# Two weight tiles at a time for the second feed-forward layer of token block A

## The reference

```python
x = x + jnp.einsum('bte,ed->btd', mix, p['w_out'])
h2 = rmsnorm(x, p['norm_ffn_g'])
u = jnp.square(jax.nn.relu(jnp.einsum('btd,df->btf', h2, p['w_up'])))   # first layer, 1024 -> 4096
x = x + jnp.einsum('btf,fd->btd', u, p['w_down'])                       # second layer, 4096 -> 1024
```

## Time and profile before

| | us |
|---|---|
| median of three runs | 1408.15 (1405.77 to 1410.62) |
| the profiled execution | 1409.37 |
| its span, first to last instruction | 1407.6 |
| PE busy | 1357.2, 96% of the span |
| PE idle ahead of its products for `dl` (line 2111) | 6.7, in 4 places |
| feed-forward of block A (eight groups) | about 488 to 990 of the span |

### The profile page before, as it was taken

The page is one execution under the profiler, slowest core; times in us unless marked ns, Lnnn a source line. Parts: engine busy times, 40 slices in busy tenths (PEclk is TensorE's granted clock), DMA queues, the critical chain, the costliest instruction groups (busy, mean ns, idle before and its releaser), DMA issues.

```text
span 1407.6 us, 23885 instructions
## 1 busy us (share of the span) xinstructions
PE 1357.2 (96%) x8589; PEld 1123.8 (80%) x8589; DVE 912.2 (65%) x1624; ACT 576.2 (41%) x1069; POOL 399.9 (28%) x395
## 2 busy tenths in 40 slices
PE   8899999999999999999999999999999999999998
PEld 6767777786777777777767767667999999999998
DVE  5459667755657787648667564535376665877875
ACT  6445333314545654523234232323444454334533
POOL 2546615335533545243000000000242212220220
PEclk9999999999999999999999999999999999999999
DMA  8547745344345564577386675874455563223021
GB/s 273 152 119 224 232 130 174 117 149 137 100 140 163 196 223 148 162 251 250 122 271 221 193 255 171 286 237 143 165 191 181 176 224 106 105 106 119 32 91 61
DMA packets 125543, 239.29 MB, mean 170 GB/s; under 512 B 13601, under 2 KB 46658, under 8 KB 125426
## 3 DMA queue, kind: packets, MB, share of 16 engines
q1 hardware_dynamic: 116226, 213.64, 46.0%
q10 hardware_dynamic: 9200, 24.13, 5.0%
HBM read 197.64 MB, written 40.09 MB: 169 GB/s over the span
## 4 chain that ended last, share of the span: by engine, by line
PE 53%; DVE 10%; ACT 4%; issue 3%; DMA 3%; SPq 1%; POOL 0%; ACTq 0%; DVEq 0%; POOLq 0%
PE ps L85 15%; PE ps L87 14%; PE ps L86 14%; PE ps L3298 2%; PE ps L1495 2%; PE ps L1532 2%; DVE fl L2788 2%; DMA raw_dn<-in_w_down 1%; PE ps L1314 1%; DVE uw_l L2018 1%; DMA vr<-in_cache_v 1%; DVE uw_l L2627 1%; DVE part_l L2826 1%; ACT uw_h L2012 1%; DVE xt L2835 1%
## 5 line engine op out<-in xcount | busy, mean ns | idle before, releaser
L3063 POOL TENSOR_TENSOR kr<-kr,qb 128x512 f32<-128x512 f32 x128 | 171.5, 1353 | 171.1 <-DMA kr<-in_cache_k 171.1
L85 PE MATMUL ps<-x2hB,uw_h 128*128 128x264 f32 (+1 forms) x512 | 145.7, 284 | 1.6 <-DVE x2lB L2850 0.7
L86 PE MATMUL ps<-x2lB,uw_h 128*128 128x264 f32 (+1 forms) x512 | 144.6, 282 | 0.0
L87 PE MATMUL ps<-x2hB,uw_l 128*128 128x264 f32 (+1 forms) x512 | 144.4, 282 | 0.0
L85 PE MATMUL ps<-part_h,fh 128*128 128x264 f32 (+1 forms) x448 | 128.7, 287 | 4.0 <-DVE xt L2835 3.7
L87 PE MATMUL ps<-part_h,fl 128*128 128x264 f32 (+1 forms) x448 | 126.9, 283 | 0.0
L86 PE MATMUL ps<-part_l,fh 128*128 128x264 f32 (+1 forms) x448 | 126.8, 283 | 0.0
L85 PE MATMUL ps<-uh,dh 128*128 128x512 f32 x256 | 105.1, 411 | 8.7 <-DVE dl L2111 6.7
L3052 DVE TENSOR_REDUCE sd<-kr 128x8 f32<-128x512 f32 x128 | 84.9, 675 | 36.9 <-POOL kr L3063 36.9
L2835 DVE TENSOR_TENSOR xt<-xt,ps 128x264 f32<-128x264 f32 (+1 forms) x224 | 86.2, 420 | 33.4 <-PE ps L87 33.1
L85 PE MATMUL ps<-x2hA,uw_h 128*128 128x512 f32 x256 | 105.2, 411 | 0.0
(11 more groups left out here) (383 smaller groups left out, 3442.7 us busy)
## 6 DMA issues: line engine op xcount, KB each, us to landing
kr<-in_cache_k SPq DMA_DIRECT2D x128, 256.0 KB, 3.2
raw_up<-in_w_up_units SPq DMA_DIRECT2D x64, 512.0 KB, 4.8
vr<-in_cache_v SPq DMA_DIRECT2D x128, 256.0 KB, 3.5
raw_dn<-in_w_down SPq DMA_DIRECT2D x32, 512.0 KB, 6.3
raw_dn<-in_w_down ACTq DMA_DIRECT2D x32, 512.0 KB, 4.7
raw<-in_w_in_units SPq DMA_DIRECT2D x23, 512.0 KB, 5.3
raw_up<-in_w_out_units SPq DMA_DIRECT2D x16, 512.0 KB, 4.2
kept_up_low<-uw_l SPq DMA_DIRECT2D x14, 512.0 KB, 6.6
```

The costliest lines, as they stand in the source:

```text
L85: pe.matmul(out, lh, rh, start=first and n == 0, stop=False, skip_group_check=onto)
L86: pe.matmul(out, lh, rl, start=False, stop=False, skip_group_check=onto)
L87: ins = pe.matmul(out, ll, rh, start=False, stop=last and n == len(ks) - 1, skip_group_check=onto)
L3063: pool.tensor_tensor(k[:, :], k[:, :], qb[v // PAGES][:, :], ALU.mult).then_inc(k_multiplied, 1)
```

## The change

The `w_down` tiles are taken two at a time. ACT makes the high parts of tiles x and x + 1 ahead of x = 0 and of x = 2 and none ahead of x = 1 and x = 3; DVE makes the low parts in the same way. `load_down` becomes `load_pair(n)`, which stands behind `split_high` of x = 0 and x = 2 and ahead of the square of the hidden tile: it loads tiles n and n + 1 (each waits for the low part of the tile two before it) and then stores the low parts of tiles n - 2 and n - 1, where before each store stood ahead of a load. The number of instructions of each kind is the same.

```diff
-        def load_down(n):
-
-            act.wait_ge(dn_low, n - 1)
+        def load_pair(n):
+
+            for i in (n, n + 1):
+                act.wait_ge(dn_low, i - 1)
+                f = i % (FT * FGROUPS) * P
+                act.dma_start(raw_dn[:, i % 2, :], a["w_down"][f:f + P, :]).then_inc(dn_in[i % 2], 16)
             if n == 2:
                 act.wait_ge(dn_out, STORED)
-            last = slice(0, HALF if (n - 2) % FT < 2 else D_MODEL)
-            if n - 2 < FT * KEPT_GROUPS:
-                act.dma_start(a["dn_low"][n - 2, :, last], dl[:, (n - 2) % FT, last].bitcast(FP32)).then_inc(dn_out, 16)
-            f = n % (FT * FGROUPS) * P
-            act.dma_start(raw_dn[:, n % 2, :], a["w_down"][f:f + P, :]).then_inc(dn_in[n % 2], 16)
+            for i in (n - 2, n - 1):
+                last = slice(0, HALF if i % FT < 2 else D_MODEL)
+                if i < FT * KEPT_GROUPS:
+                    act.dma_start(a["dn_low"][i, :, last], dl[:, i % FT, last].bitcast(FP32)).then_inc(dn_out, 16)
...
             for x in range(FT):
                 t = KT + FT * g + x
-                if x:
-                    load_down(FT * g + x + 1)
-                down_high(g, x)
+                if x % 2 == 0:
+                    down_high(g, x)
+                    down_high(g, x + 1)
                 beside(tick + 2 * x)
...
                 if x + 1 < FT and t > KT:
                     split_high(act, t + 2)
+                if x % 2 == 0:
+                    load_pair(FT * g + x + 2)
                 i = up_no(g, x)
...
             for o in range(KT):
-                if o == 0:
-                    load_down(FT * g + FT + 1)
                 beside(tick + 2 * FT + o)
...
                 beside(tick + 2 * x)
-                down_low(g, x)
+                if x % 2 == 0:
+                    down_low(g, x)
+                    down_low(g, x + 1)
```

## The result

| | before | after |
|---|---|---|
| median, us | 1408.15 (5 runs) | 1417.72 (1415.78 to 1420.43, 5 runs) |
| the profiled execution | 1409.37 | 1415.78 |
| its span | 1407.6 | 1414.1 |
| PE waits for `dl`, 480 to 1000 us | 6.7 in 4 places | none |

The changed kernel is slower: 1.0063 of before, interval 1.0048 to 1.0077 (the two medians of the table alone give 1.0068). The forecast was 1407.2 in a range of 1402.6 to 1411.5. The kernel lost 9.6 us between the medians and 6.4 between the two profiled executions; the profiled one of after was the fastest of its five.

What follows compares the result with a forecast made beforehand. PE, busy 96% of the span, bounds the kernel; its dl waits put 6.7 us at stake. Groups' gains and losses (-1.0, -0.85, +1.55, 0, +1.3) sum to 1.0 us faster: 1408.4 profiled, 1407.2 median, range 1402.6 to 1411.5.

Steps and rivals of the forecast that it cites:

- the ledger of groups 0 and 1: Forecast as seen by PE: group 0 loses 1.0 us (late attention copy), group 1 loses 0.85 us.
- step 2: Pair at x = 0: DVE's extra dl is covered; in group 0 the norm comes 1.1 us later, taken as 0 net.
- group 1's two delays: Group 1: 0.75 us at the score product, 0.95 at the attention product; 1.7 lost against 1.36 won.
- step 1: Head of down in groups 1, 2, 3, 5: PE's wait for the low part goes; up to 6.7 us back.
- step 3: Pair at x = 2, groups 0 to 3: DVE's relu, split_low and hidden low part come 1.14 us later.
- step 4: Four ACT issues before the square, groups 0 to 3: 0.6 to 0.75 us uncovered; at x = 2, 1.75 us later altogether.
- the estimate: Shared DVE/POOL port lock: 0.85 us more at x = 2 of groups 0, 1, 2, making the sum about 1.5 slower.
- Slower: ACT is held at x = 2: Rival, groups 0 to 3: ACT's queued work waits, 10 us lost against at most 5.6 back; 1412.6 us, chance 0.10.
- Most of it comes back: Rival: most of the 6.7 us of dl waits returns, 5.6 us in groups 1, 2, 3, 5; 1402.6 us, chance 0.18.
- the order of the transfers: Rival that only transfer order matters: early loads shorten nothing; no time of its own, lies in the forecast, no separate chance.

Runs made afterwards that it cites:

- run 6: Kernel before; only DVE's low part of tile 3 moved ahead of the side jobs of x = 3, groups 1 to 7; 1411.33 us, ratio 1.0007.
- run 8: Kernel before; tile 3's split put behind the hidden tile of x = 2 in groups 2 to 7, in group 1 DVE's low part before side jobs; 1412.63 us.
- run 1: Changed kernel with load_pair moved behind the hidden tile's copy and the side jobs, splits still in pairs; 1418.2 us, ratio 1.0051.
- run 3: Changed kernel with pairs only for tiles 0 and 1, tiles 2 and 3 as before; 1412.91 us, ratio 1.0023 to the kernel before.
- run 7: Changed kernel plus unused matmuls (14, 18, 18, 18 calls) ahead of four waiting products in groups 0 and 1; 1417.44 us, ratio 1.0063.
- run 9: Changed kernel plus unused matmuls (7, 9, 9, 9 calls) ahead of four waiting products in groups 0 and 1; 1418.31 us, ratio 1.0063.
- run 2: Changed kernel with each store again ahead of its load, at the changed place; 1416.88 us, ratio 1.0058.
- run 13: Changed kernel with group 0 as before and pairs from group 1 on; 1413.41 us, ratio 1.0023 to the kernel before.
- run 4: Changed kernel with pairs only for tiles 2 and 3, tiles 0 and 1 as before; 1413.79 us, ratio 1.0028 to the kernel before.
- run 12: Changed kernel with pairs in groups 2, 4, 5, 6, 7 only, plus seven unused matmuls in the wait at 512 us; 1409.88 us, ratio 1.0011.
- run 5: Changed kernel with groups 0 and 1 as before and pairs from group 2 on; 1409.51 us against 1409.46, ratio 1.0002.
- run 10: Changed kernel with pairs in groups 2, 4, 5, 6 and 7 only, the others as before; 1407.66 us, ratio 0.9993.

## Why the prediction was wrong, step by step

The sum forecast a gain of 1.0 us; the block lost 7.2. The step that failed is the ledger of groups 0 and 1: with step 2's "0 net" and group 1's two delays side by side it forecast -1.85, and the traces show -8.1. Beside it, group 1's 1.36 us from step 1 were counted as won and were not. By group, in the profiled executions (the measured numbers are differences between the starts of the first-layer products of one group and the next):

| group | forecast | measured | what differs |
|---|---|---|---|
| 0 | -1.0 | -2.7 | the attention copy is 3.3 later, not 1.75 |
| 1 | -0.85 | -5.5 | chain of ACT and DVE later at each turn, residual add, clock |
| 2 | +1.55 | +0.5 | 2.1 at the head, 1.6 lost in its `down` |
| 3 | 0 | -1.1 | `ul` wait of 2.29 (1.1 forecast), clock behind it |
| 5 | +1.3 | +1.1 | as said |
| 4, 6, 7 | 0 | +0.3 | |

**Step 1 was right in what it says and wrong in what it is worth.** The wait for `dl` is gone everywhere. But runs 6 and 8 take it away by other means and gain nothing, because the residual add, which hangs on POOL's products with the cached keys, is next: in run 6 the `dl` waits fall by 5.0 us and those for `xt` rise by 5.4. Group 1's 1.36 us are not worth 1.36. The prediction saw this wait and let it keep its place; it had to be moved up with PE.

**Step 2 asked the wrong engine.** The 1.1 us at the norm came (2.10 - 0.88 = 1.22), but not by DVE, where the norm "stands behind" the pair: DVE's first step of the norm began 8.4 us after the start of the first-layer products, before 8.6. It came by POOL. Timelines of DVE and POOL, before and then after:

```profile
494.98 0.27 POOL L1608 TENSOR_SCALAR stat<-stat 128x1 f32<-128x1 f32 x1
...
498.71 2.01 POOL L2104 TENSOR_TENSOR norm<-norm,half 128x4 f32<-128x4 f32 x1 [1.23 <-DVE norm L2116]
```

```profile
495.05 2.35 DVE L2113 TENSOR_TENSOR dl<-raw_dn,dh 128x1024 fp32r<-128x1024 f32 x2
495.06 2.47 POOL L1608 TENSOR_SCALAR stat<-stat 128x1 f32<-128x1 f32 x1
...
498.47 1.95 POOL L3067 TENSOR_TENSOR kr<-kr,qb 128x512 f32<-128x512 f32 x1
500.37 1.01 POOL L2106 TENSOR_TENSOR norm<-norm,half 128x4 f32<-128x4 f32 x1
```

A small POOL instruction that began with the pair ended with it, after 2.47 us instead of 0.27, and POOL's part of the norm, behind it and a key product, ended 12.1 us after the start instead of 10.9. In runs 1, 3, 7 and 9 the same instruction took 2.17 to 2.39 us; in run 2 a key product came first, and the pair took 3.18. In runs 6 and 13, with group 0 as before, it took 1.12, and the norm waited 1.41 and 1.31 us.

The prediction set these 1.1 us against the wait at 512.44, "0 net". For PE that came true: the wait at 512.44 and the slow product behind it are gone, and PE stood ready for the next attention product at 33.9 us against 34.1. But the copy that this product needs comes out of ACT and DVE, and DVE began the `dl` of x = 2 at 519.68 - 489.26 = 30.4 us instead of 519.04 - 489.85 = 29.2. Ahead of that `dl` DVE has idle time of its own (1.66 us, before 1.62), and it absorbed nothing, for the sum there waits for POOL, and POOL for a page of keys. The sums behind the norm began at 19.2 us instead of 17.4, SP's page loads wait for them, and SP issued the one for that page at 22.8 instead of 20.9. I let idle time of PE absorb a delay that ran on along DVE, SP and POOL. Run 3, which has the norm late and x = 2 as before, shows it without the second `dl`: its `dl` begins 30.3 us after the start, and the copy ends 34.4 us after it, 1.1 later than before.

```profile
520.49 1.22 DVE L2130 TENSOR_TENSOR dl<-raw_dn,dh 128x1024 fp32r<-128x1024 f32 x1
...
523.99 0.58 ACT L1567 ACTIVATE attn_t<-ps 128x512 f32<-128x512 f32 x1
```

What it costs PE beside the pair at x = 2 is less: `down` of group 0 starts 0.5 us later than before in run 3, 2.4 in run 4 and 2.7 with both.

**Steps 3 and 4 were right in mechanism.** Of the 3.3 us at group 0, 1.2 are the later start of the `dl`, 1.15 the second `dl` and 1.0 the issues (step 4 said 0.6). Run 4, with the norm as before, has the `dl` 0.7 us late and the copy 3.1, so not all of the 1.2 is the norm's; POOL's product, which waits for the page of cached keys, stands ahead of it. Step 4's figure at x = 0 is to be seen in group 1. Timeline of ACT:

```profile
577.38 0.82 ACTq L2036 DMA_DIRECT2D raw_dn<-in_w_down  x2
578.24 0.94 ACTq L2042 DMA_DIRECT2D kept_dn_low<-dl  x2
579.22 0.63 ACT L2083 ACTIVATE xr<-xr 128x512 f32<-128x512 f32 x1 [0.80 <-issue]
```

0.80 against 0.75 forecast, and the wait for `p1b` grew by 0.91 (1.75 to 2.66). By the times of run 1 the issues are not the larger part.

**The sum over group 1 failed.** The forecast put two delays beside each other and took the 1.36 off them. In the trace they follow one another on one chain, from which PE's gain at `down` takes nothing off: the attention copy of 600 comes 5.5 us later from the start than before (110.6 against 105.1): 2.7 carried from group 0, 0.9 by the issues, 0.95 by the second `dh`, and 1 us by the hidden tile's low part at 591.89 below, which was in no step.

```profile
591.36 1.73 POOL L3067 TENSOR_TENSOR kr<-kr,qb 128x512 f32<-128x512 f32 x1 [1.26 <-DMA kr<-in_cache_k]
...
591.89 1.74 DVE L2158 TENSOR_TENSOR ul<-xr,uh 128x512 fp32r<-128x512 f32 x1
...
597.06 2.00 ACT L2029 ACTIVATE dh<-raw_dn 128x1024 fp32r<-128x1024 f32 x2
...
599.45 3.43 DVE L2113 TENSOR_TENSOR dl<-raw_dn,dh 128x1024 fp32r<-128x1024 f32 x2
...
599.93 2.29 PE L1532 MATMUL ps<-vb,attn_t 128*128 128x128 f32 x9 [2.75 <-ACT attn_t L1567]
600.02 1.77 POOL L3067 TENSOR_TENSOR kr<-kr,qb 128x512 f32<-128x512 f32 x1 [6.94 <-DMA kr<-in_cache_k]
```

The low part of the hidden tile took 1.74 us instead of 0.68, and the two `dl` 3.43 instead of 2.35, each with one of POOL's products beside it. Rows like these are what the prediction weighed a rule against. By that rule, the exclusive lock on the shared port pair (the Trainium skill, SBUF — State Buffer, the section SBUF: two separate sides), the trace agrees in this group; of the three places where the estimate charged 0.85 us, only group 1 shows about 1 (3.43 - 2.35). Groups 0 and 2 took 2.35 and 2.52. The other kernels with a pair at these places say how steady that is: 3.42 to 3.44 us in group 1 in all six, 2.35 in group 0 in all five, and 2.38 to 3.92 in group 2 in nine. In group 2 the charge thus came in some kernels and not in others; the longest pair there stood ahead of the longest wait at the head of `down` (3.92 and 1.66 us, run 1). At x = 0 of group 0, where the estimate charged nothing, POOL was the one held. POOL's products had moved against DVE's work, because both engines were later by different amounts.

**The clock was in no step.** Longer waits came with more stretches at the lower clock. It looks like 4 of the 7 us, and runs 7, 9 and 12 show that taking most of it out in groups 0 and 1 gives nothing back in the time. It isn't an addend to the waits, where the chain of another engine sets the next product; in `down` of group 1 up to 1.7 us of it may be real.

**The rivals.** "Slower: ACT is held at x = 2" had the right mechanism, places and sign, at 0.10: forecast 1412.6, measured 1417.7. It charged 10 us against 5.6 us won back. The charges in groups 2 and 3 hardly came, those of groups 0 and 1 came whole, with the norm on top (8.1 us against 5.0), and of the 5.6 only 0.5 in group 2 and 1.1 in group 5 were won. "Most of it comes back" falls with runs 5, 6 and 10. That the order of the transfers doesn't count is borne out by run 2. The point from which the slower one decides, an attention loop with less slack than 2.5 us, was met by every row quoted (0.8 at 523.94, none at 581.47 and 595.00); the evidence for a much higher chance stood in the earlier trace rows.

What stays open: the last 1 to 2 us in groups 1 and 3, where a longer wait and a lower clock behind it come together, and why the residual add inside `down` of group 2 is 0.8 us late. No run parts POOL's share from the rest, by moving its instructions away from the pairs; it is read from the rows alone.

## What to carry to other kernels

A wait of the busiest engine is worth what is left when the next wait behind it is moved up by the same amount; try that alone, with the smallest edit, before paying for it elsewhere. A delay on a feeding engine is not absorbed by idle time of the engine that waits for it at the end, and idle time on its own chain helps only if what ends it doesn't start later too. Beside a hand-ordered side job that already holds the main engine at every turn, an instruction put ahead of it can cost its full duration at each turn, as in groups 0 and 1 here, and the delays add along the chain. A pair can also hold a third engine and what is queued there, as it held POOL here (2.47 us instead of 0.27).

## What was not expected of the hardware

The granted clock doesn't fall after every long wait. In after it fell behind waits of 2.10, 2.75, 2.12 and 2.29 us, and not behind 2.79 (at 525.92) and 2.66 (at 584.48). The wait of 1.85 or 1.86 us at about 512 brought it down in before and in runs 5, 8 and 10, but not in runs 6 and 13, where the 14 products behind it took their 1.83 us:

```profile
512.73 1.83 PE L1532 MATMUL ps<-vb,attn_t 128*128 128x128 f32 x14 [1.85 <-ACT attn_t L1567]
```

At the lower level matmuls of 128x512 followed each other by 0.43 us instead of 0.23. Timeline of PE of after, behind the norm:

```profile
504.89 0.63 PE L86 MATMUL ps<-x2lA,uw_h 128*128 128x512 f32 x1
505.32 0.63 PE L87 MATMUL ps<-x2hA,uw_l 128*128 128x512 f32 x1
```

A plain fp32 matmul call of 128x128 leaves two records: seven calls in run 9 are the 14 in this row, 0.25 us a call.

```profile
502.00 1.72 PE L1941 MATMUL ps<-ident,ones 128*128 128x128 f32 x14
```
